# First groups of both attention layers get their own order of work; rope swap from the unscaled projection

## The reference

```python
for i in range(DEPTH):                       # DEPTH = 2
    h = rmsnorm(x, norm_mix[i])
    if i % 2 == 0:   # differential attention, 8 heads, rotary
        q, k = rope(h @ Wq), rope(h @ Wk); v = h @ Wv
        a = softmax(q1 k1 / 8) - lam * softmax(q2 k2 / 8)     # chunk-causal mask
        o = rmsnorm(a @ v, subln) * (1 - lam_init)
    else:            # Fox: 16 heads, no rotary, causal, with forget gates
        logf = log_sigmoid(h @ Wf + b); c = cumsum(logf)
        s = q k / 8 + c_q - c_k; o = softmax(s) @ v
    x = x + o @ Wo
    x = x + (silu(g @ Wgate) * (g @ Wup)) @ Wout              # g = rmsnorm(x, norm_ffn[i])
y = rmsnorm(x, norm_final)
```

## Time and profile before

| | |
|---|---|
| runs shown | 1520.25, 1521.70, 1523.22 us; median 1521.7 |
| profiled execution | 1521.43 us, span of its instructions 1519.6 |
| busy | PE 97%, ACT 42%, DVE 40%, POOL 47% |
| mean granted clock of TensorE | 0.991 |
| differential attention | to about 330 us |
| its feed-forward part | to about 748 us |
| Fox attention | to about 1087 us, its group a period of some 32.45 us |
| second feed-forward part and final norm | to the end |

### The profile page before, as it was taken

How to read it: one execution, slowest core, us unless ns; L and a number is a source line. 1 busy time by engine, 2 the same in 40 slices (tenths; PEclk the granted TensorE clock), 3 DMA queues, 4 the chain that set the end, 5 groups by cost and what they waited for, 6 DMA issues and landing times.

```text
span 1519.6 us, 30293 instructions
## 1 busy us (share of the span) xinstructions
PE 1480.3 (97%) x10911; PEld 1458.2 (96%) x10911; DVE 605.4 (40%) x1122; ACT 632.2 (42%) x1102; POOL 717.2 (47%) x873
## 2 busy tenths in 40 slices
PE   6999999999999999999989999999999999999996
PEld 5999999999999999999979999999999999999996
DVE  6667766451111111111267878774511111111112
ACT  5677777352222222222336666663422222222211
POOL 4554455355555555545523233333455555554442
PEclk9999999999999999999999999999999999999998
DMA  4222222122222222222322222221222222222222
GB/s 175 79 91 64 85 79 85 56 70 83 83 83 83 83 83 79 77 84 83 111 65 68 88 64 78 64 83 56 83 80 78 80 81 83 83 79 85 83 89 74
DMA packets 41559, 123.79 MB, mean 81 GB/s; under 512 B 4624, under 2 KB 9232, under 8 KB 41504
## 3 DMA queue, kind: packets, MB, share of 16 engines
q1 hardware_dynamic: 41504, 123.06, 24.5%
HBM read 111.21 MB, written 11.83 MB: 81 GB/s over the span
## 4 chain that ended last, share of the span: by engine, by line
PE 94%; DVE 3%; issue 1%; ACT 1%; POOL 1%; DMA 0%; SPq 0%; DVEq 0%; ACTq 0%
PE ps L504 80%; PE ops L620 3%; PE sps L557 3%; PE tps L577 2%; PE ops L610 1%; PE sps L559 1%; PE sps L563 1%; PE sps L565 1%; POOL w_lo L1134 1%; DVE acc L1256 1%; PE tps L591 0%; DVE xT L1265 0%; PE ops L627 0%; PE sps L685 0%; PE sps L525 0%
## 5 line engine op out<-in xcount | busy, mean ns | idle before, releaser
L1134 POOL TENSOR_TENSOR w_lo<-w_raw,w_hi 128x256 fp32r<-128x256 f32 x780 | 580.8, 776 | 699.4 <-ACT w_hi L810 699.4
L504 PE MATMUL ps<-xh,w_hi 128*128 128x288 f32 x2176 | 483.4, 304 | 21.9 <-DVE xl L1538 10.6
L504 PE MATMUL ps<-xh,w_lo 128*128 128x288 f32 x2176 | 467.9, 297 | 0.0
L504 PE MATMUL ps<-xl,w_hi 128*128 128x288 f32 x2176 | 467.4, 297 | 0.0
L810 ACT ACTIVATE w_hi<-w_raw 128x1024 fp32r<-128x1024 f32 (+1 forms) x200 | 208.6, 1043 | 418.9 <-PE ps L504 415.9
L504 PEld LDWEIGHTS ps<-xh,w_hi 128*128 128x128 f32 x2176 | 348.3, 190 | 26.0 <-issue 24.0
L504 PEld LDWEIGHTS ps<-xh,w_lo 128*128 128x128 f32 x2176 | 352.2, 190 | 0.0
L504 PEld LDWEIGHTS ps<-xl,w_hi 128*128 128x128 f32 x2176 | 351.7, 189 | 0.0
L504 PE MATMUL ps<-hl,w_hi 128*128 128x288 f32 x704 | 151.0, 295 | 0.0
L504 PE MATMUL ps<-hh,w_hi 128*128 128x288 f32 x704 | 151.0, 295 | 0.0
L504 PE MATMUL ps<-hh,w_lo 128*128 128x288 f32 x704 | 150.9, 295 | 0.0
(11 more groups left out here) (171 smaller groups left out, 1750.2 us busy)
## 6 DMA issues: line engine op xcount, KB each, us to landing
w_raw<-w_units SPq DMA_DIRECT2D x184, 512.0 KB, 3.2
w_raw<-w_units SPq DMA_DIRECT2D x16, 384.0 KB, 2.9
xT<-x_in SPq DMA_DIRECT2D x8, 288.0 KB, 6.2
dk_out<-kf SPq DMA_DIRECT2D x8, 288.0 KB, 2.1
dv_out<-vf SPq DMA_DIRECT2D x8, 288.0 KB, 4.1
fk_out<-kf SPq DMA_DIRECT2D x8, 288.0 KB, 4.0
fv_out<-vf SPq DMA_DIRECT2D x8, 288.0 KB, 4.1
y_out<-yt SPq DMA_DIRECT2D x8, 288.0 KB, 2.3
```

The source lines that it names most:

```text
L504: mm = nc.tensor.matmul(out[:, half, :], w[:, k, :], rhs[:, kt, half * HALF:(half + 1) * HALF], start=start and w is w_hi[slot] and rhs is ...
L1134: part = nc.gpsimd.tensor_tensor(w_lo[slot][:, k:k + 2, :], w_raw[slot][:, k:k + 2, :], w_hi[slot][:, k:k + 2, :].bitcast(F32), ALU.subtract)
```

## The change

Five edits, most of them to the start of the differential layer, and new order tables for Fox.

1. **Preparing x.** ACT makes all eight squares, behind all `xh`; POOL makes none. DVE adds them behind all `xl`. ACT splits unit 1 behind `xh` of tile 5 rather than 6.
2. **Norm sum 0** stands ahead of slice 7 of unit 1 and goes to `ops` (512 columns) and `tps` (64 columns) instead of `sps`, so that the logarithm is two ACT instructions.
3. **Swap of group 0** copies straight from the accumulator once the unit is done (`w_used`), before DVE takes it; DVE's take waits for the swap instead. q's swap goes to `osq`, k's to `qsw`. `rope_done` becomes two semaphores, one for k and one for q.
4. **v of group 0** accumulates in `sps`; its unit waits for no accumulator. Group 1's k waits for k and q of group 0 to be read; the first score waits until v has been read.
5. **Tables of their own** (`ACT_ONE`, `DVE_ONE`, `POOL_ONE`) give the order of projection work of group 0 in both layers, and of what of it falls into group 1.
6. **Fox's tables** for all other groups are replaced; the differential layer's keep all but `SS` (115 becomes 114).

```diff
 PE_AT = {
-    FOX: dict(S=[5, 11, 16, 18, 26, 38, 41, 48, 61, 68], T=[20, 26, 32, 39, 52, 55, 65, 74, 84, 93], PVS=[30, 66],
-               PVP=[54, 101], VT=15, SS=-1)}
+    FOX: dict(S=[5, 11, 16, 18, 28, 32, 45, 48, 61, 65], T=[20, 26, 32, 43, 52, 55, 61, 73, 84, 93], PVS=[30, 68],
+               PVP=[54, 101], VT=16, SS=-1)}
 ACT_AT = {
-    FOX: dict(EXP=[5, 8, 16, 24, 34, 38, 53, 53, 65, 73], P=[15, 24, 29, 40, 45, 55, 71, 76, 84, 94], V=13, OS=[25, 66],
-               OSH=[45, 71], O=[53, 94], SCALE=-1, OH=-1, W=[31, 72, 97], SWAP=[], KH=43, KH2=85, QH=81)}
+    FOX: dict(EXP=[5, 8, 19, 24, 37, 38, 53, 53, 65, 73], P=[13, 22, 27, 41, 43, 53, 65, 73, 74, 84], V=10, OS=[25, 71],
+               OSH=[47, 74], O=[60, 97], SCALE=-1, OH=-1, W=[31, 71, 97], SWAP=[], KH=42, KH2=84, QH=76)}
 DVE_AT = {
-    FOX: dict(MAX=[1, 9, 11, 12, 27, 32, 43, 47, 59, 62], W=[10, 11, 17, 24, 39, 50, 52, 60, 60, 81], P=[16, 22, 29, 41,
-               49, 55, 69, 77, 82, 87], OS=[37, 65], OSL=[53, 74], OL=[54, 96], NORM=-1, SPLIT=-1, K=25, RK=-1,
-               KL=50, Q=72, RQ=-1, QL=83, AUG=89, V=89)}
+    FOX: dict(MAX=[1, 9, 11, 12, 29, 38, 39, 47, 59, 62], W=[10, 11, 17, 24, 39, 50, 52, 61, 61, 82], P=[16, 22, 32, 41,
+               49, 55, 65, 76, 83, 88], OS=[48, 77], OSL=[56, 81], OL=[60, 100], NORM=-1, SPLIT=-1, K=34, RK=-1,
+               KL=51, Q=71, RQ=-1, QL=92, AUG=83, V=94)}
 POOL_AT = {
-    FOX: dict(OSQ=-1, VL=12, SIN=[], W=[66, 70, 96])}
+    FOX: dict(OSQ=-1, VL=4, SIN=[], W=[7, 10, 35])}
+ACT_ONE = {
+    DIFF: dict(W=[10, 32, 94], SWAP=[15, 22], KH=56, KH2=-1, QH=44, F=-1, N=17),
+    FOX: dict(W=[52, 58, 95], SWAP=[], KH=41, KH2=94, QH=81, F=57, N=-1)}
+DVE_ONE = {
+    DIFF: dict(K=20, RK=71, KL=87, Q=20, RQ=29, QL=85, AUG=-1, V=38, F1=-1, F2=-1),
+    FOX: dict(K=35, RK=-1, KL=44, Q=65, RQ=-1, QL=94, AUG=89, V=102, F1=55, F2=62)}
+POOL_ONE = {
+    DIFF: dict(SIN=[13, 25], W=[0, 37, 53]),
+    FOX: dict(SIN=[], W=[5, 30, 87])}
-NORM0_AT = 3
+NORM0_AT = 7
...
+        def tile_of(n):
+            return sps[:, :, 0:HALF] if n.it is None and n.c == 2 else proj(n.c % 2)
+        def first(g):
+            return g.it is None and g.c == 0
+        def swapped_half(g, which):
+            return osq if first(g) and which else qsw
...
-                    if some(n - 1):
+                    if some(n - 1) and not (n.it is None and n.c in (2, 3)):
                         pe.wait_ge(ps_read, val(n - 1))
+                    if n.it is None and n.c == 3:
+                        pe.wait_ge(ps_read, 2)
...
+                if i == 0:
+                    nc.tensor.matmul(ops[:], ones, acc[:, 0:SEQ], start=True, stop=True)
+                    nc.tensor.matmul(tps[:, 0, 0:NEW], ones, acc[:, SEQ:T], start=True, stop=True).then_inc(ss_done, 1)
+                    return
...
             def swap(g, n, which, quadrants):
-                act.wait_ge(ps_read, val(n + 1))
-                if some(g * 2 + which):
-                    act.wait_ge(rope_done, val(g * 2 + which))
+                if first(g):
+                    act.wait_ge(w_used, which + 1)
+                else:
+                    act.wait_ge(ps_read, val(n + 1))
+                    if which:
+                        act.wait_ge(rope_done[0], val(g + 1))
+                    else:
+                        act.wait_ge(rope_done[1], val(g))
...
-                if k % 2 or k == 6:
-                    nc.scalar.activation(sq_all[:, k, :], xT[:, k, :], ACT.Square).then_inc(sq_act, 1)
-                if k == 6:
+                if k == 5:
                     lead(Num(0))
+            for k in range(KT):
+                nc.scalar.activation(sq_all[:, k, :], xT[:, k, :], ACT.Square).then_inc(sq_act, 1)
...
-            for k in (0, 2, 4):
-                pool.wait_ge(x_loaded[k], 16)
-                nc.gpsimd.tensor_tensor(sq_all[:, k, :], xT[:, k, :], xT[:, k, :], ALU.mult).then_inc(sq_pool, 1)
...
-                if k >= 3:
-                    add_square(k - 2)
-            add_square(KT - 2)
-            add_square(KT - 1)
+            for k in range(1, KT):
+                add_square(k)
```

More of the change, by code:

```diff
@@ L305, in encoder @@
         part_done = sem("part_done")
-        rope_done = sem("rope_done")
+        rope_done = [sem(f"rope_done{which}") for which in range(2)]
         kh_done = sem("kh_done")
@@ L549, in score @@
                     pe.wait_ge(exp_done, val(J - 1))
+                elif L == DIFF and a.it is None and a.c == 0:
+                    pe.wait_ge(ps_read, 3)
                 if jj == 0:
@@ L653, in attention, with group @@
                         pv_prompt(L, a, h)
-            def group(L, g, par, first=False):
+            def group(L, g, par, second=False):
                 u, n = g * 3 + U_LAYER * L, g * 3 + N_LAYER * L
                 for tick in range(TICKS):
-                    if not first:
+                    if not second:
                         attention(L, g - 2, par, tick + TICKS)
@@ L752, in _ @@
                 first_group(L)
-                group(L, Num(1), 1, first=True)
+                group(L, Num(1), 1, second=True)
                 with pe.Fori(0, 3) as it:
@@ L1008, in project, with group @@
                     k_hi_again(g, par)
-            def group(L, g, par, first=False, alone=False):
+            def group(L, g, par, second=False, alone=False):
                 for tick in range(TICKS):
-                    if not alone and not first:
+                    if not alone and not second:
                         attention(L, g - 2, par, tick + TICKS)
@@ L1020, in group @@
                         scale_of_norm(2)
-                    if alone and L == DIFF and tick == 0:
+                    if alone and tick == ACT_ONE[L]["F"]:
+                        forget()
+                    if alone and tick == ACT_ONE[L]["N"]:
                         scale_of_norm(0)
-                    if alone and L == FOX and tick == 52:
-                        forget()
-                    project(L, g, par, tick)
+                    project(L, g, par, tick, (ACT_ONE if alone else ACT_AT)[L])
             def forget():
@@ L1167, in project, with group @@
                         lead(g * 3 + (U_LAYER * L + i + 1))
-            def group(L, g, alone=False, first=False):
+            def group(L, g, alone=False, second=False):
                 if alone and L == FOX:
@@ L1178, in group @@
                         attention(L, g - 1, tick)
-                        project(L, g - 1, tick + TICKS)
-                    project(L, g, tick)
+                        project(L, g - 1, tick + TICKS, (POOL_ONE if second else POOL_AT)[L])
+                    project(L, g, tick, (POOL_ONE if alone else POOL_AT)[L])
             pool.wait_ge(w_hi_done, 1)
@@ L1190, in _ @@
                 group(L, Num(0), alone=True)
-                group(L, Num(1), first=True)
+                group(L, Num(1), second=True)
                 with pool.Fori(0, 3) as it:
@@ L1278, in take_k @@
                     dve.wait_ge(kh_done, val(gi))
+                if L == DIFF and first(g):
+                    dve.wait_ge(ps_swapped, 1)
                 take(kf[:, 0:T], g * 3 + (U_LAYER * L + 1), g * 3 + N_LAYER * L, (cosr if L == DIFF else rs)[:])
@@ L1283, in take_q @@
                     dve.wait_ge(qh_done, val(g + G * L))
+                if L == DIFF and first(g):
+                    dve.wait_ge(ps_swapped, 2)
                 take(qf[:], g * 3 + (U_LAYER * L + 2), g * 3 + (N_LAYER * L + 1), (cosr if L == DIFF else rs)[:])
@@ L1526, in add_square @@
             def add_square(k):
[L1528 to L1529 removed]
+                dve.wait_ge(sq_act, k + 1)
                 if k == 1:
```

64 lines of the change are left out of this document (33 added, 31 removed).

## The result

The changed kernel took 1512.6 us in the median of seven runs (1505.5 to 1514.6), the kernel before 1523.1 beside it (1520.3 to 1524.9): ratio 0.9922, 95% interval 0.9898 to 0.9947, or 11.9 us less on the 1521.7 of the prediction (1509.8). The two medians alone differ by 10.4. Forecast were 7.0 less, with a range from 1511.4. Why the first series came out larger is most of what this study found.

What follows compares the result with a forecast made beforehand. TensorE, busy 97% of 1519.6 us, bounds the kernel; only its idle or lower-clock time can be won. Differential start 6.5, Fox's first group 0, steady groups 0.5: 7.0 less, 1514.7 us, range 1511.4 to 1518.8.

Steps and rivals of the forecast that it cites:

- The first unit: Differential start: without squares between the xh, unit 0 ends near 18.0 instead of 20.7, 2.7 us won.
- no contention: Lower bound, 16.3 us, on the start of unit 0's last slice, forecast for 17.2, if DVE and POOL do not collide.
- Norm and swap: Differential start: norm sum at 23.6, hidden by unit 1; rs at 26.4; unit 2 follows at 25.5, its 2.9 us stall gone.
- w_lo of unit 3: Differential start: POOL begins it at 31.0, takes 3.9, ends at 34.9; unit 3 starts at 35.0 instead of 41.86.
- q's and k's low parts: DVE ahead of the first differential score: q's low part about 36.5, k's at 38.1 us.
- Rival 2: Four DVE operations behind q's rotation, and w_lo, each pay 0.5; first score at 40; 3.5 us won, 1518.2; chance 0.17.
- The first score: Differential layer: starts at about 38.2 instead of 44.55, 6.3 us won, bounds 4.5 and 7.4.
- the 2.9 that the prediction had named: Stall of 2.9 us for k's swap ahead of unit 2, gone because unit 2 has an accumulator of its own.
- Fox's first group: Reordered low parts, AUG and v; waits of 2.5 and 1.7 us stay; 0 won, between -0.5 and +0.5.
- a slow stretch behind the differential gap: Less work at the lower clock behind the first differential score: 0.2 us won, between 0 and 0.4.
- Fox's steady groups: New order removes the third transpose's 0.40; DVE's queue takes most back; 0.5 us won, between -2 and +2.9.
- Around the span: Execution time outside the profiled span: 1.8 us, kept unchanged in the forecast.

Runs made afterwards that it cites:

- the start alone: Changed kernel with every Fox table, its first group's too, set back to the order before; only the differential start changed: median 1514.7 us, ratio 0.9955.
- the kept-busy kernel: Kernel before plus three unused matrix products in each gap ahead of differential units 2 and 3 and Fox's unit 3: 1519.5 us, ratio 0.9985.

## Why the prediction was right or wrong

**The step that failed** is in its first paragraph: "Only time in which TensorE stands still, or runs at its lower clock, can be won", with 418.00 us of 418.00 from 330 to 748 us taken as a fixed cost. The profiled execution won 6.84 us in just that stretch, with TensorE always busy and at granted clock 1.00. Nothing shows this to be an effect of the change: two further profiles of the same kernel have the old 423.6 there, the kernel before has quick times too, and one of another kernel had the quick stretch elsewhere. But three of the seven runs compared were such executions, against none of the seven of before, and so the result came to 11.9 us less, where the usual executions differ by 7.4 and 7.0 were forecast. The range had no term for it. What sets the quicker pace stays open.

**The first unit.** Forecast end 18.0, measured 17.23 by the start of unit 1 less its wait. The forecast had xl7 as the limit, at 17.2. xl7 did take the 1.30 beside POOL that it was given, but ended at 15.82: x tile 5 was there at 11.36 and not at 12.01 "whatever the order" (ACT began xh5 at 11.0 to 12.0 in the thirteen profiles). TensorE, whose first four slices took 1.44 to 1.58 each against 0.80 later, started the last slice at 16.29 without a wait: its own pace was the limit, at the bound that the prediction calls "no contention". Unit 1 then waited 0.54 for w_lo, a wait that the sum had not named (4.46 us of POOL from 13.16), so that 0.23 remained.

**Norm and swap.** Norm sum forecast 23.6, measured 23.44; unit 1's end 25.5, measured 25.35; the logarithm of 64 columns 0.25, measured 0.31; rs 26.4, measured 26.33; swap of q done 28.9, measured 28.97. Unit 2 had no gap. These points are right, but one of them by luck: w_lo of unit 2 was priced at 2.9, less than any of the rows of w_lo in the earlier trace rows, and took 4.39 beside DVE's sums. That it was still ready, at 24.54, is because x came earlier and ACT's squares followed each other at 0.58 us instead of 0.67, so that ACT was 1.9 ahead of the forecast (k's swap done at 22.7, forecast 24.6). With the split where the forecast had it and the measured 4.39 it would have come at 26.5, about 1 late.

**w_lo of unit 3.** Forecast 31.0 to 34.9 and TensorE at 35.0; measured 30.97 to 34.80 and 34.89. Its price, 3.9, was taken between two rows of before, by what runs beside it, and measured 3.83.

**q's and k's low parts.** k's low part was forecast for 38.1 and came at 37.30. The four operations of DVE behind q's rotation took 0.75, 1.30, 2.04 and 1.09. Two paid some 0.5 us: k's rotation (758 ns in the earlier trace rows) and the first half of q's low part (1.27; the second half, behind the end of w_lo, took 0.76). v, from PSUM, paid nothing. k's low part, with two inputs in SBUF, took the 1.09 that it takes with POOL idle: it began at 36.21, just ahead of the next w_lo, and this time it was POOL that waited, 1.58 for a quarter that takes 0.72 to 0.74 alone:

```profile
36.31 1.58 POOL L1172 TENSOR_TENSOR w_lo<-w_raw,w_hi 128x256 fp32r<-128x256 f32 x1 [1.51 <-ACT w_hi L837]
```

Rival 2, in which all four pay, fell. The Trainium skill, "SBUF — State Buffer", section "Who interferes with whom", has the one of such a pair that issues second wait until the other's instruction is finished; the profile agrees on both sides (1.30 for DVE's rotation, 1.58 for POOL's quarter). To price a chain by it one has to ask for each link whether POOL is at work and who was first.

**The first score**: 38.2 forecast, 37.89 measured. Two slices took 3.0 and not 2.7, and the score waited for nothing. In the other two profiles of the changed kernel the slices were done sooner and it waited 0.8 and 0.55 for k's low part, to 37.98 and 37.45: the two ends lie side by side, as forecast. 6.66 won of 6.3 forecast, and 7.0 at the end of the layer where the sum had 6.5. The mechanism is right; that the amounts agree so closely is in part luck, as the 44.55 that they start from is the earliest of three profiles (46.25 and 46.12 in the others), and the closing norm sum differs by 4.9 to 8.6 between single profiles of the two kernels, 7.2 in the mean of three and three. Two experiments undo its two largest parts: the squares are worth 2.66 at the first score for the 2.7 forecast; the third accumulator 4.2, for the 2.9 that the prediction had named.

**Fox's first group**, costed at 0 between -0.5 and +0.5: the two waits were 2.4 and 1.0 for 2.5 and 1.7, and the first score came as late as before, 31.28 behind the gates. But 1.84 were won behind it (1.6 to 1.9 in the three profiles of each), as the stretch at 1.2 GHz was over before the score and not behind it. The prediction gave a slow stretch behind the differential gap a term, and behind Fox's none; the start alone gave the same gain with Fox's old order. The term was mis-sized, by 1.8; the kept-busy kernel shows that a clean clock is worth 1.4 to 1.6 there.

**Fox's steady groups**: forecast 0.5 between -2 and +2.9, measured -0.05 to +0.04, and 0.17 at the end. The 0.40 of the earlier trace rows went as said, and the prompt's product kept its own, as counted. What the count missed is the new 0.49 behind the last transpose.

**Around the span** the sum kept the 1.8 us of before. In all 24 runs of the changed kernel the time is 2.2 to 2.35 above the span, in the kernel before 1.75 to 1.9, and with the squares put back 1.8 again: 0.45 of what the span wins is lost there, and it comes with the new preparation of x. What it is, the profile, which covers the span alone, doesn't show.

## What to carry to other kernels

Where a kernel's bound engine is at 97%, work out the few places where it stands still, to the tenth, by counting each queue through: the times at which TensorE started or waited held within some 0.3 us here, but for the end of unit 0, and that although one price behind them was 1.5 too low. So check the terms, and not only the landmarks. Take the landmarks from several executions of the same kernel: here the first score of the kernel before moved by 1.7 between profiles. Then, when an execution differs from the forecast, first cut both spans at the same landmarks, and look whether the difference lies where the change is; matmuls per 100 us of full work is the quickest test. And when a link of a chain is moved forward, look at once at the link that is then last: with q's high part alone moved, v's transpose came 35.7 us behind Fox's gates (34.0 in the changed kernel), with its low part moved too 31.1 and 32.7.

## What the hardware showed that was not expected

- TensorE, always busy and at granted clock 1.00, ran the same 128x288 matmuls at 752 per 100 us or at 771 to 772, changing between and within executions of one kernel. A stretch of some 270 us at the quicker pace is worth 6.8 us. What sets the pace stayed open: in the windows of 100 us shown neither the granted clock nor DMA's share differs (0.24 or 0.25 at either pace).
- Nine useless products, three in each of three gaps, made the kernel before some 2.5 us shorter (0.9 to 3.8).
- The stretch at 1.2 GHz behind a gap of 2 to 3 us is not the same in executions of one kernel: behind the differential gap of the unaltered changed kernel it covered unit 3's two slices, or nothing, or some 7 us from 36.2 on, over the scores. In Fox's first group it lasted from 782.95 to 789.7, idle time included, in the kernel before, and was absent in the start alone.
- Of a DVE operation with two SBUF inputs and a POOL operation beside it, the one that started second took longer: k's rotation 1.30 for 0.76, and a quarter of w_lo 1.58 for 0.73 when DVE had started 0.1 earlier.
